# Gated feed-forward of a float32 transformer kernel: up-projections in chunks of 512 columns by seven products of quarters

## The reference, cut to what matters

```python
def swiglu(x, w1, w3, w2):
    return (jax.nn.silu(x @ w1) * (x @ w3)) @ w2

def second_block(x, ffn1_norm, ffn1_w1, ffn1_w3, ffn1_w2, mix_norm, ...):
    h = x
    h = h + 0.5 * swiglu(rms_norm(h, ffn1_norm[l]), ffn1_w1[l], ffn1_w3[l], ffn1_w2[l])
    ...
    h = h + 0.5 * swiglu(rms_norm(h, ffn2_norm[l]), ffn2_w1[l], ffn2_w3[l], ffn2_w2[l])
```

## Time and profile before

| | |
|---|---|
| median of 3 runs | 2319.98 us (2315.99 to 2324.92) |
| profiled execution: time, span | 2314.78 us, 2313.0 us |
| TensorE busy | 96% of the span |
| VectorE, ScalarE, GpSimd busy | 51%, 36%, 8% |
| granted TensorE clock, mean | 0.986 |
| GLU1, from chunk 0's second half to the end | about 1205 to 1561 us |
| GLU2, the same | about 1942 to 2300 us |

### The profile page before, as it was taken

One profiled execution on the slowest core, in us unless ns is written; L12 is line 12 of the kernel. 1 busy time (PEld: TensorE's weight loads), 2 busy tenths in 40 slices (PEclk: granted clock), 3 DMA queues, 4 the chain that ended last, 5 costly groups with the idle time before them and its releaser, 6 DMA issues.

```text
span 2313.0 us, 27926 instructions
## 1 busy us (share of the span) xinstructions
PE 2228.9 (96%) x11611; PEld 1886.9 (82%) x11611; DVE 1173.9 (51%) x1845; ACT 825.9 (36%) x1241; POOL 179.8 (8%) x155
## 2 busy tenths in 40 slices
PE   6998999999999899999999999999999999999998
PEld 3877988888897788888898888887778889888887
DVE  5676566556577664334353433344664445333334
ACT  3555342213256543223243222234443324222222
POOL 7210000000033000000020000002012001000000
PEclk8999999999999999999999999999999999999999
DMA  6442255555520222322313232224112331422320
GB/s 230 141 140 85 93 171 180 190 180 185 189 74 19 86 80 91 109 91 91 110 55 110 91 109 91 82 73 120 57 32 73 119 110 56 127 92 92 109 73 37
DMA packets 144099, 245.45 MB, mean 106 GB/s; under 512 B 4763, under 2 KB 69622, under 8 KB 143846
## 3 DMA queue, kind: packets, MB, share of 16 engines
q1 hardware_dynamic: 139216, 228.02, 29.7%
q0 software_dynamic: 4096, 15.28, 2.0%
q10 hardware_dynamic: 662, 0.37, 0.1%
HBM read 241.56 MB, written 2.10 MB: 105 GB/s over the span
## 4 chain that ended last, share of the span: by engine, by line
PE 88%; DVE 6%; ACT 3%; issue 1%; DMA 1%; POOL 0%; SPq 0%; DVEq 0%; ACTq 0%
PE PS L66 87%; ACT t L72 3%; DVE t L83 2%; DVE t L86 1%; DVE t L75 1%; PE PS L69 1%; DMA t<-in_w_ada_dram 1%; DVE t L79 1%; POOL t L75 0%; DVE t L92 0%; DVE t L80 0%; SPq L101 0%; DVE t L95 0%; ACT L72 0%; DVEq L58 0%
## 5 line engine op out<-in xcount | busy, mean ns | idle before, releaser
L66 PE MATMUL PS<-t,t 128*128 128x512 f32 (+4 forms) x11244 | 2180.0, 357 | 53.3 <-ACT t L72 16.3
L66 PEld LDWEIGHTS PS<-t,t 128*128 128x128 f32 (+2 forms) x11244 | 1844.1, 188 | 386.2 <-issue 61.3
L72 ACT ACTIVATE t<-t 128x2048 fp32r<-128x2048 f32 (+10 forms) x551 | 527.7, 972 | 1174.0 <-PE PS L66 691.3
L75 DVE TENSOR_TENSOR t<-t,t 128x2048 fp32r<-128x2048 f32 (+8 forms) x476 | 581.9, 1227 | 650.9 <-ACT t L72 648.8
L72 ACT ACTIVATE t<-PS 128x512 f32<-128x512 f32 (+5 forms) x307 | 162.3, 545 | 183.0 <-PE PS L66 123.5
L75 POOL TENSOR_TENSOR t<-t,t 128x512 f32<-128x512 f32 (+2 forms) x71 | 88.1, 1242 | 1136.7 <-ACT t L72 962.7
L83 DVE SCALAR_TENSOR_TENSOR t<-t,t,t 128x1024 f32<-128x1024 f32 (+2 forms) x149 | 140.5, 947 | 16.4 <-DMA t<-in_w_ada_dram 10.9
L72 ACT ACTIVATE t<-t,t 128x256 fp32r<-128x256 f32 (+5 forms) x212 | 112.4, 537 | 88.9 <-DVE t L83 45.7
L75 DVE TENSOR_TENSOR t<-t,PS 128x512 f32<-128x512 f32 (+2 forms) x92 | 54.6, 600 | 147.2 <-PE PS L66 140.8
L83 DVE SCALAR_TENSOR_TENSOR t<-PS,t,t 128x512 f32<-128x512 f32 (+3 forms) x120 | 76.9, 643 | 94.6 <-PE PS L66 84.7
L69 PE MATMUL PS<-t,t 128*128 128x128 f32 (+1 forms) x367 | 57.8, 296 | 26.9 <-DMA t<-in_x_dram 6.1
(11 more groups left out here) (30 smaller groups left out, 154.2 us busy)
## 6 DMA issues: line engine op xcount, KB each, us to landing
t<-in_w_ff_dram SPq DMA_DIRECT2D x64, 1024.0 KB, 5.3
t<-in_ffn_w_dram SPq DMA_DIRECT2D x60, 1024.0 KB, 5.2
t<-in_w_ada_dram SPq DMA_DIRECT2D x36, 1024.0 KB, 6.1
t<-in_w_in_dram SPq DMA_DIRECT2D x13, 1024.0 KB, 5.0
t<-in_w_ada_dram POOLq DMA_DIRECT2D x24, 512.0 KB, 4.4
t<-in_swa_w_qkv_dram SPq DMA_DIRECT2D x6, 1024.0 KB, 5.9
t<-in_ffn_w_dram SPq DMA_DIRECT2D x8, 768.0 KB, 4.2
t<-in_w_in_dram SPq DMA_DIRECT2D x24, 256.0 KB, 3.6
```

What stands on the lines that cost most here:

```text
L66: return Instr(self.real and self.real.matmul(o, lhs, rhs, start=start, stop=stop, **more))
L72: return Instr(self.real and self.real.activation(o, src, func, **more))
L75: return Instr(self.real and self.real.tensor_tensor(o, a, b, op))
```

## The change

Chunk 0 (256 columns of w1 and of w3) stays as it was. The other 2560 hidden columns become 5 chunks c = 1..5 of 512. For a chunk, w1 (gate 0) and w3 (gate 1) are each a **unit**. A unit is the product of a [1024 x 512] weight with the [1024 x 512] activations; both are cut into 2 x 2 quarters, and the four result quarters come from **seven products of quarters**, m = 0 to 6, instead of eight. A product is 2 row tiles x 4 k-steps x 3 = 24 matmuls of 256 tokens. So a unit is 168 matmuls of 256 tokens, where it was 96 of 512.

Its operands are sums of quarters. Of the activations, four sums are made once per layer (`dve_t_sum` three, `pool_t_sum` one) and split (`act_t_hi`, `dve_t_lo`); for this the normed activations are kept in float32 (`H32`), in place of the two temporaries. Of the weights, each unit needs four sums of 128x1024 elements: m = 1 and 4 on GpSimd (`pool_sum`), m = 2 and 3 on VectorE (`dve_sum`; each of these two is built on the sum before it). All seven operands are then split in halves of the old buffers (`UH`, `UL`; six places, item w takes that of w-6), in 7 + 7 instructions of 128x1024 where 2 + 2 of 128x2048 did. Both raw halves of a unit must have landed before its sum 1; the first raw buffer is given back at the low part of m = 4, the second at that of m = 6.

In PSUM a unit has three banks x, y, z. `act_keep` copies x (after m = 0), y (after m = 1) and x again (after m = 2) to SBUF, while TensorE goes on adding to x and y; `dve_join` adds y after m = 3, x after m = 4 and z after m = 5 to the copies. The fourth quarter stays in x. Then silu (`act_take`, gate 0), or the multiplication (`dve_times`) and the split of the hidden layer (`act_take`, `dve_low`, gate 1), by quarters. The w2 blocks now are 6, 8 and 8 tiles, after the chunks 1-2, 3-4 and 5.

```diff
+        def unit(name, w, n0):
+            p0, w0 = len(PLAN), len(WT)
+            WX.setdefault(name, []).append(w0)
+            for m in range(7):
+                WT.append(dict(kt=4, nc=256, parts=None, wide=256, p=p0 + (m > 0), m=m, u=(p0, p0 + 1)))
+            for half, last in ((0, 4), (1, 6)):
+                LOADS[len(PLAN)] = (w[:, 4 * half:4 * half + 4, n0:n0 + 512], 4, 512, False)
+                PLAN.append(("w", w0 + last))
...
+        def dve_lo_seven(e, w):
+            m = WT[w]["m"]
+            a11, a12, _, a22 = quarters(w)
+            if m in (1, 2):
+                dve_sum(e, w + 1, m + 1)
+            e.wait_ge(hi, w)
...
+        def pool_sum(e, w0, m):
...
+            if m == 1:
+                e.tensor_tensor(dst, a21, a22, ALU.add).then_inc(summed, w)
+            else:
+                e.tensor_tensor(dst, a11, a21, ALU.subtract).then_inc(summed, w)
...
+            e.wait_for(banks.free((u, "x")))
+            product(0, "x", *of_h(0, 0), True)
+            e.wait_for(banks.free((u, "y")))
+            product(1, "y", *of_t(1), True)
+            e.wait_ge(copied, (u, 1))
+            product(2, "x", *of_t(2), False)
+            e.wait_ge(copied, (u, 3))
+            product(3, "y", *of_h(1, 1), False)
+            e.wait_ge(copied, (u, 2))
+            product(4, "x", *of_t(3), False)
+            e.wait_for(banks.free((u, "z")))
+            product(5, "z", *of_h(1, 0), True)
+            e.wait_ge(joined, (u, Q22))
+            e.wait_ge(t_lo, (i, 4))
+            product(6, "x", quarter_h(HHI, 0, 1), quarter_h(HLO, 0, 1), False)
...
+        def act_unit(e, i, c, gate):
+            u, w0 = (i, c, gate), g_unit(i, c, gate)
+            act_split(e, AHEAD[w0] - 1)
+            act_keep(e, u, 1, 0, "x", Q11)
...
+        def dve_unit(e, i, c, gate, nm):
...
+            dve_split(e, AHEAD[w0 + 3] - 1)
+            dve_join(e, u, 3, "y", Q12, 2)
+            dve_split(e, AHEAD[w0 + 4] - 1)
+            dve_times(e, u, Q12)
+            dve_join(e, u, 4, "x", Q22, 3)
+            dve_split(e, AHEAD[w0 + 5] - 1)
+            dve_times(e, u, Q22)
+            dve_low(e, u, Q12)
+            dve_join(e, u, 5, "z", Q11, 1)
+            dve_split(e, AHEAD[w0 + 6] - 1)
+            dve_times(e, u, Q11)
+            dve_low(e, u, Q22)
+            dve_low(e, u, Q11)
+            dve_times(e, u, Q21)
+            dve_low(e, u, Q21)
```

More of the change, by code:

```diff
@@ new lines, in dve_sum @@
+        def dve_sum(e, w, m):
+            a11, a12, _, _ = quarters(w)
+            dst, last = UL32[AT[w]][:, :, :], UL32[AT[w - 1]][:, :, :]
+            for before in AFTER[w]:
+                e.wait_ge(acc, ("used", before))
+            for p in WT[w]["u"]:
+                e.wait_ge(landed[SLOT[p]], p)
+            if m == 2:
+                e.wait_ge(summed, w - 1)
+                e.tensor_tensor(dst, last, a11, ALU.subtract).then_inc(summed_dve, w)
+            else:
+                e.wait_ge(summed_dve, w - 1)
+                e.tensor_tensor(dst, a12, last, ALU.subtract).then_inc(summed_dve, w)
@@ new lines, in pool_sum @@
+        def pool_sum(e, w0, m):
+            w = w0 + m
+            a11, _, a21, a22 = quarters(w)
+            dst = UL32[AT[w]][:, :, :]
+            for before in AFTER[w]:
+                e.wait_ge(acc, ("used", before))
+            for p in WT[w]["u"]:
+                e.wait_ge(landed[SLOT[p]], p)
+            if m == 1:
+                e.tensor_tensor(dst, a21, a22, ALU.add).then_inc(summed, w)
+            else:
+                e.tensor_tensor(dst, a11, a21, ALU.subtract).then_inc(summed, w)
@@ new lines, in act_gate @@
+        def act_gate(e, i, hf):
+            s = g_slot(i, 0)
+            for n in range(2):
+                k1, k3 = (("g", i), 0, n, hf), (("g", i), 1, n, hf)
+                ta.take(k3, (hid_lo, k3))
+                tm = TMP[ta[k3]][:, COLS[hf]]
+                e.wait_ge(acc, k1)
+                e.wait_for(ta.free(k3))
+                e.activation(tm, PS[:, banks[k1], COLS[hf]], ACT.Silu).then_inc(relu, k1)
+                e.wait_ge(sqr, k3)
+                e.activation(GH[s][:, n, COLS[hf]], tm, ACT.Copy).then_inc(hid_hi, k3)
@@ new lines, in bass_two_blocks, with pe_unit, product, of_h @@
+        Q11, Q12, Q21, Q22 = (0, 0), (0, 1), (1, 0), (1, 1)
+        def pe_unit(e, i, c, gate, nm):
+            u, w0 = (i, c, gate), g_unit(i, c, gate)
+            taken = sqr if gate else relu
+            banks.take((u, "x"), (taken, (u, Q21)), keep=True)
+            banks.take((u, "y"), (joined, (u, Q12)), keep=True)
+            banks.take((u, "z"), (joined, (u, Q11)), keep=True)
+            def product(m, name, bh, bl, first):
+                w = w0 + m
+                e.wait_ge(hi, w)
+                e.wait_ge(lo, w)
+                b = banks[u, name]
+                for n in range(2):
+                    for k in range(4):
+                        cs = slice(128 * n, 128 * n + 128)
+                        o = PS[:, b, 256 * n:256 * n + 256]
+                        ah, al = whi(w)[:, k, cs], wlo(w)[:, k, cs]
+                        e.matmul(o, ah, bh[:, k, :], start=first and n == k == 0, stop=False, skip_group_check=True)
+                        e.matmul(o, ah, bl[:, k, :], start=False, stop=False, skip_group_check=True)
+                        t = e.matmul(o, al, bh[:, k, :], start=False, stop=k == 3, skip_group_check=True)
+                t.then_inc(acc, (u, m), ("used", w))
+            def of_h(r, t):
+                for k in range(4 * r, 4 * r + 4):
+                    e.wait_ge(h_hi, (nm["N"], k, t))
+                    e.wait_ge(h_lo_pool if k % 2 else h_lo, (nm["N"], k, t))
+                return quarter_h(HHI, r, t), quarter_h(HLO, r, t)
+            def of_t(n):
+                e.wait_ge(t_lo, (i, n))
+                return TH[n - 1], TL[n - 1]
+            e.wait_for(banks.free((u, "x")))
[13 more added lines that the diff above has]
+            product(6, "x", quarter_h(HHI, 0, 1), quarter_h(HLO, 0, 1), False)
+            for name in "xyz":
+                banks.open((u, name))
@@ new lines, in g_of, with xs @@
+        def g_of(i, blk):
+            tiles = [[(0, 0), (0, 1)] + [(1, t) for t in range(4)], [(c, t) for c in (2, 3) for t in range(4)],
+                     [(c, t) for c in (4, 5) for t in range(4)]][blk]
+            def xs(e, k, n, hf):
+                c, t = tiles[k]
+                for h in halves_of(hf):
+                    if c == 0:
+                        e.wait_ge(hid_lo, (("g", i), 1, t, h))
+                    else:
+                        e.wait_ge(hid_lo, ((i, c, 1), (t // 2, h)))
+                s = g_slot(i, c)
+                return GH[s][:, t, COLS[hf]], GL[s][:, t, COLS[hf]]
+            return xs
```

425 lines of the change are left out of this document (299 added, 126 removed).

## The result

The changed kernel takes **2333.95 us** (median of 4 runs, 2332.33 to 2334.91) against 2318.32 for the kernel before in the same session: ratio 1.0062, 95% interval 1.004 to 1.0084. It is 0.6% slower, where 0.3% faster was forecast, and lies inside the range at its upper end (2290 to 2336).

What follows compares the result with a forecast made beforehand. TensorE's matmul pitch was taken to bound the kernel. Matmuls -32.0, norm -3.0, hand-overs +10.7, first units +10.9 and +5.5 sum to -7.9 us: 2312 us from 2319.98, range 2290 to 2336.

Steps and rivals of the forecast that it cites:

- Matmuls, -32.0: In 20 units, 168 matmuls at 120 ns replace 96 at 226.7 ns, 1.6 us less each: -32.0 us.
- Norm, -3: Norm before the first unit: float32 kept for all tiles shortens TensorE's waits, 2 us in GLU1, 1 in GLU2: -3 us.
- Hand-overs, +10.7: After gate-1 units of chunks 1 and 3, TensorE waits for ScalarE's copy of x, 2.5 us (3.2 at GLU1's first): +10.7 us.
- just in time: Unit after a late hand-over: the join that product 6 needs is done at 27.7 us against 28.45.
- First units, +10.9 and +5.5: First unit of each stage: late sums, low parts and joins make TensorE wait, +10.9 us in GLU1, +5.5 in GLU2.
- The wait that I named as the longest: Sign of being right: the longest wait stands before product 4 of GLU1's first unit, on VectorE.
- would break the sum itself: Sign of being wrong: a pitch other than 120 ns, or a granted clock that falls at each wait.
- lock: Port shared by GpSimd and VectorE: a GpSimd sum stops VectorE's instructions with two SBUF inputs for up to 2.4 us.
- The slack absorbs it: Rival: GpSimd's sums fall into VectorE's idle times or do not stop it; 2294 us, chance 0.25.
- VectorE becomes the bound of every pair: Rival: VectorE's work, holds and waits make 44.1 us per pair against 43.5 before; 2339 us, chance 0.20.

Runs made afterwards that it cites:

- e9_all: Changed kernel with all weight sums on VectorE, earlier load, x copied first at hand-overs, late rescalings and chunk 0's operand splits moved earlier: 2297.05 us, ratio 0.9907.
- e6_load: Changed kernel, with the load into a unit's first raw half held only until that half's last sum and a11's low part: 2328.05 us, ratio 1.0035.
- e4_rescale: Changed kernel, with the eight rescalings of X moved to just ahead of the first w2 block's residual additions: 2327.82 us, ratio 1.0041.
- e2_fill: Changed kernel, with matmuls of ones filling TensorE's idle time ahead of waits in the first units and at the hand-overs: 2329.44 us, ratio 1.0055.
- e3_nopool: Changed kernel without GpSimd's two weight sums per unit, raw quarters used instead, so the output is not the reference's: 2297.55 us, ratio 0.9917.
- e5_dvesums: Changed kernel, with all four weight sums of a unit on VectorE and none on GpSimd: 2315.08 us, ratio 0.9984.
- e1_act: Changed kernel, with ScalarE's copy of x put ahead of two high parts at the four hand-overs: 2336.35 us, ratio 1.0082.

## Why the prediction was wrong, step by step

- **Matmuls, -32.0:** right. The pitch of 120 ns holds inside every run (168 in 20.41 us, 2204 in 313.75 in e9_all).
- **Norm, -3:** -1.9 in idle time. GLU1's 1.30 us for silu stayed (1.28), one tile later, since VectorE's new sums of activations stand ahead of chunk 0's first multiplication. In GLU2 two drops of the clock at 1948 us took the rest in this execution; others of the same instructions had none.
- **Hand-overs, +10.7:** the place, the engines and the chain were right, the size was not: 14.6. Two things were missing. GpSimd's sum for product 1 is itself held (3.29 us), and VectorE then waits for it; I had only let it hold others. At the second hand-over this idle time, 1.63 us, less the 0.40 already lost before product 6, is about the excess of 3.80 over 2.5. And the sum had no term for product 6 of the gate-1 units of chunks 1 and 3, which waited 0.4 to 0.7 us each (+2.2) until e6_load brought the load earlier. The product 6 that I had called "just in time", in the unit behind a hand-over, was in time.
- **First units, +10.9 and +5.5:** 8.6 and 7.2, together 15.9 for 16.4. GLU1's rescalings were in the sum, and e4_rescale took back what they cost; GLU2's longest wait (5.96) stood before product 1, where I had 2.5. So the total is near by luck in part: GLU1 was 2.3 us under its forecast, GLU2 1.7 over. The wait that I named as the longest, before product 4 of GLU1's first unit, was 3.24; five of the other twelve were longer.
- **The step that failed is the one without a line in the sum: the clock.** I named a drop at each wait as something that "would break the sum itself", had a row that showed it, and still costed the drops at nothing. Eleven more of them at 1.5 us are 16.5 us gross. On the profiled executions the sum gave 2306.9; with 16.5 for these drops, 5.6 by which the waits were too small (32.7 against 27.1), 1.1 from the norms, 2.1 in the unchanged stage and 2.1 that stay unexplained it is 2334.3, the profiled time. The median forecast of 2312 is missed by 22. Some 5 us of the way from 2306.9 to 2334 may belong to the execution and not to the change: two drops at GLU2's norm and the unchanged stage.
- **But the clock was not the root.** e2_fill took most drops away and gained 4.5 us. Without the drops the waits alone would have left about 2312 + 5.6 + 1, no change; what makes both is the sums on GpSimd. The term behind it is the "lock": my sum gave GpSimd's holds 18.0 us (hand-overs 10.7 against 0.4 without them, first units and load 16.4 against 8.7), e3_nopool shows 36.4 for the sums with all that follows from them.
- **The rivals.** "The slack absorbs it" (2294) described the kernel without GpSimd's sums: e3_nopool is at 2297.6 with idle times of 10.3 us, where it had 9.1. "VectorE becomes the bound of every pair" came near in time (2339), but not in mechanism: TensorE did not wait in every unit, and with more work of its own VectorE was faster (e5_dvesums, e9_all). I had counted a hold as work, 31.7 + 9.6 us; a hold also falls at a moment that nobody chose, and two runs (e1_act, e2_fill) show it 2 us dearer for a shift of 1.5 us.

## What to carry to other kernels

A second engine that shares a port is no free helper. Here GpSimd took 40 additions of 1.22 us off VectorE and cost it 62 us, so they were best done on VectorE. When a chain is late, price the idle time of TensorE together with the clock drop that follows it, but don't add them blindly: a TensorE that is earlier can wait longer at the next place, and can start another engine's work at a worse moment. And where a single edit only moves a wait from one place to the next, try the edits together before the theory is dropped: here three gave -9.6 us one by one, and -25.0 at once with the copy first in the first units too.
